# Projecting r and k of ten RWKV pairs with seven half products, from weight sums that transfers add up in device memory

## The reference, cut to what matters

```python
h = rmsnorm(x, g_pre)
p_shift, q_mem, gate = jnp.split(h @ w_in, RWKV_SPLITS, axis=-1)   # r, k, v (12 x 128 columns each), two small ones
prev = jnp.concatenate([shift_prev, p_shift[:, :-1]], axis=1)
s = p_shift + (prev - p_shift) * mu
r, k, v, wl, al = jnp.split(s, SHIFT_SPLITS, axis=-1)
...
y, wkv = wkv_recurrence(r_h, decay, k_mod, v_h, kk, a, wkv0)       # per head of 64
```

## Time and profile before

| | before |
|---|---|
| median of 3 runs | 1682.9 us |
| profiled execution / its span | 1686.12 / 1684.4 us |
| TensorE matmul busy | 1619.8 us (96%) |
| VectorE busy | 1022.2 us (61%) |
| ScalarE busy | 399.7 us (24%) |
| DMA | 419.97 MB, mean 249 GB/s |

### The profile page before, as it was taken

One profiled execution on the slowest core, in us unless ns is written; L12 is line 12 of the kernel. 1 busy time (PEld: TensorE's weight loads), 2 busy tenths in 40 slices (PEclk: granted clock), 3 DMA queues, 4 the chain that ended last, 5 costly groups with the idle time before them and its releaser, 6 DMA issues.

```text
span 1684.4 us, 28149 instructions
## 1 busy us (share of the span) xinstructions
PE 1619.8 (96%) x9704; PEld 1293.7 (77%) x9704; DVE 1022.2 (61%) x5017; ACT 399.7 (24%) x1011; POOL 160.8 (10%) x295
## 2 busy tenths in 40 slices
PE   7999999899999999998999989999999999999998
PEld 6667776677777777666996877777777777788997
DVE  4777455664555556435865376777777777432755
ACT  2122111211121212121112243333333333221012
POOL 1112211122122222221000000000000000020000
PEclk9999999999999999999999999999999999999999
DMA  9689999999999999998326043333333323365441
GB/s 382 247 318 395 416 408 401 363 387 420 412 406 420 419 409 413 403 382 340 118 88 257 30 158 123 104 104 104 104 104 104 104 85 113 119 255 193 151 159 52
DMA packets 102158, 419.97 MB, mean 249 GB/s; under 512 B 41844, under 2 KB 46464, under 8 KB 92416
## 3 DMA queue, kind: packets, MB, share of 16 engines
q0 software_dynamic: 41680, 218.91, 32.7%
q1 hardware_dynamic: 54264, 189.70, 29.8%
q10 hardware_dynamic: 6072, 9.56, 1.5%
HBM read 405.28 MB, written 12.85 MB: 248 GB/s over the span
## 4 chain that ended last, share of the span: by engine, by line
PE 77%; DVE 9%; DMA 7%; ACT 4%; issue 2%; POOLq 1%; POOL 0%; SPq 0%; ACTq 0%; DVEq 0%
PE psum L765 24%; PE psum L1203 11%; PE psum L837 10%; PE psum L819 6%; PE psum L1063 5%; DMA kvr<-in_cv 4%; PE psum L754 3%; PE psum L804 2%; PE psum L1250 2%; DMA kvr<-in_ck 1%; DVE arena L2403 1%; DVE kvr L1997 1%; PE psum L788 1%; PE psum L776 1%; ACT gT L1833 1%
## 5 line engine op out<-in xcount | busy, mean ns | idle before, releaser
L1997 DVE CUSTOM_DVE_ANT_0 kvr<-kvr,arena 128x128 f32<-128x128 f32 x1488 | 323.6, 288 | 110.5 <-DMA kvr<-in_ck 110.3
L765 PE MATMUL psum<-hT,wring 128*128 128x264 f32 x1536 | 363.5, 393 | 0.0
L765 PEld LDWEIGHTS psum<-hT,wring 128*128 128x128 f32 x1536 | 291.0, 193 | 67.4 <-issue 19.8
L1203 PE MATMUL psum<-hT,kvr 128*128 128x264 f32 x1152 | 283.9, 391 | 0.0
L1203 PEld LDWEIGHTS psum<-hT,kvr 128*128 128x128 f32 x1152 | 211.5, 190 | 34.4 <-issue 1.1
L1997 DVE DVE_READ_ACCUMULATOR2_ANT arena<- 128x1 f32 x1488 | 123.8, 83 | 0.0
L819 PE MATMUL psum<-hT,kvr 128*128 128x264 f32 x512 | 121.9, 389 | 0.0
L819 PEld LDWEIGHTS psum<-hT,kvr 128*128 128x128 f32 x512 | 94.6, 190 | 15.4 <-issue 0.4
L1063 PE MATMUL psum<-kvr,arena 128*32 128x384 f32 x1024 | 99.8, 505 | 5.4 <-DMA kvr<-in_cv 5.4
L699 POOL DMA_DIRECT2D kvr<-in_cv x128 | 67.7, 529 | 376.9 <-PE psum L1063 307.7
L699 POOL DMA_DIRECT2D kvr<-in_ck x128 | 67.6, 528 | 218.2 <-issue 217.5
(11 more groups left out here) (447 smaller groups left out, 2288.5 us busy)
## 6 DMA issues: line engine op xcount, KB each, us to landing
kvr<-in_ck POOLq DMA_DIRECT2D x128, 768.0 KB, 11.8
kvr<-in_cv POOLq DMA_DIRECT2D x128, 768.0 KB, 11.1
kvr<-in_wrkv SPq DMA_DIRECT2D x12, 3072.0 KB, 13.5
kvr<-in_wo SPq DMA_DIRECT2D x14, 2048.0 KB, 8.3
wring<-in_wkv SPq DMA_DIRECT2D x12, 2048.0 KB, 11.9
wring<-in_wm SPq DMA_DIRECT2D x8, 2048.0 KB, 12.5
wring<-in_wg SPq DMA_DIRECT2D x8, 2048.0 KB, 12.2
kvr<-in_wg SPq DMA_DIRECT2D x8, 2048.0 KB, 9.1
```

What stands on the lines that cost most here:

```text
L765: last = mm(psum[:, m % 2, 0:n], w[:, k, t * P:(t + 1) * P], rhs[:, k, 0:n], start=(k == 0), stop=(k == KT - 1))
L1203: last = mm(psum[:, m % 2, 0:T], w[:, k, t * P:(t + 1) * P], hT[:, k, :], start=(k == 0), stop=(k == KT - 1))
L1997: last = v_.tensor_tensor_reduce(page, page, qb[:, n % 2, h * P:(h + 1) * P], 1.0, 0.0, ALU.mult, ALU.add, S[:, n % 2, j * FH + h:j * FH + ...
```

## The change

For pairs 2 to 11 (turns 0 to 9), r and k are no longer two tiles of 16 k tiles and 264 columns. The weight block [first or second eight k tiles] x [r, k] and the inputs [k half] x [132-column half] form two 2x2 block matrices, multiplied with seven products of eight k tiles by 132 columns: R11, RS2, R12, RS1, RS4, RS3, R22. The v tile stays whole, in parts of 4, 4, 4, 2 and 2 k tiles. The seven products and five value parts are the twelve `project_part`s of a turn.

The four weight sums per pair are made by GpSimd's queue in device memory (`wsums`): four copies of 512 KB, then four adding transfers (`accum_op`) of 512 KB, three steps of which wait for the one before. Then nine half tiles of 512 KB (five from the weights in pieces of 512 bytes, four from the sums) are loaded by the same queue into a ring of twelve slots, instead of 3 MB by SyncE's. The sums of two pairs are made right after the last page of layer 0, the others two pairs ahead.

VectorE makes the four input sums once (in the place of the residual stream, which is stored to `xkept` and loaded back in turn 10), and in each turn joins products in five steps of 132 columns. ScalarE's copies are placed anew.

```diff
+SP0 = 2
+NSP = RP - SP0
+R11, RS2, R12, RS1, RVL, RS4, RS3, RVH, R22 = range(9)
+RSLOTS, RW1 = 12, 8 * P
...
 # SyncE
+            sp.wait_ge(sem("x_new"), len(RESIDUAL))
+            sp.dma_start(xkept, xT[:, :, :].rearrange("p k t -> p (k t)")).then_inc(sem("x_in2"), 16)
...
-                if o == RP - 3:
-                    late_unit(0)
                 if o == RP - 2:
                     late_unit(1)
                     late_unit(2)
-                if o + 3 < RP:
-                    sp.wait_ge(sem("p_done"), M_RKV + 3 * (o + 2))
-                    pair(o + 3, "wrkv", runit[:, (o + 1) % 2, :], f"proj_in{(o + 1) % 2}")
+                    sp.wait_ge(sem("x_in2"), 32)
+                    sp.dma_start(xT[:, :, :].rearrange("p k t -> p (k t)"), xkept).then_inc(sem("x_in2"), 16)
...
 # GpSimd
+            def sums_copied(i):
+                w = pair_weights(i)
+                for n, (k, x) in enumerate(((0, 1), (0, 0), (0, 0), (8, 0))):
+                    pool.dma_start(sum_at(i, n), w[:, k:k + 8, x, :]).then_inc(sem("rk_sum"), 16)
+            def sums_added(i, part):
+                w = pair_weights(i)
+                pool.wait_ge(sem("rk_sum"), 16 * (8 * i + (4, 6, 7)[part]))
+                if part == 0:
+                    pool.dma_start(sum_at(i, 0), w[:, 8:16, 1, :], accum_op=ALU.add).then_inc(sem("rk_sum"), 16)
+                    pool.dma_start(sum_at(i, 2), w[:, 0:8, 1, :], accum_op=ALU.add).then_inc(sem("rk_sum"), 16)
+                elif part == 1:
+                    pool.dma_start(wsums[i][:, 1, :], wsums[i][:, 0, :], accum_op=ALU.add).then_inc(sem("rk_sum"), 16)
+                else:
+                    pool.dma_start(wsums[i][:, 3, :], wsums[i][:, 1, :], accum_op=ALU.add).then_inc(sem("rk_sum"), 16)
+            def ring_load(i, j):
+                g = 9 * i + j
+                if g < RSLOTS:
+                    pool.wait_ge(sem("p_done"), M_RKV + 3 * (g // 6 + 1))
+                else:
+                    pool.wait_ge(sem("rk_mm"), g - RSLOTS + 1)
...
+            for i in range(NSP):
+                ring_load(i, R11)
+                if i + 2 < NSP:
+                    sums_copied(i + 2)
+                for j in (RS2, R12, RS1):
+                    ring_load(i, j)
+                if i + 2 < NSP:
+                    sums_added(i + 2, 0)
+                for j in (RVL, RS4, RS3):
+                    ring_load(i, j)
+                if i + 2 < NSP:
+                    sums_added(i + 2, 1)
+                for j in (RVH, R22):
+                    ring_load(i, j)
+                if i + 2 < NSP:
+                    sums_added(i + 2, 2)
...
 # TensorE
+                def half_product(j, out, x, first=True, last=True):
+                    w = ring_item(o, j).rearrange("p (k n) -> p k n", k=8)
+                    pe.wait_ge(*ring_full(o, j))
+                    for k in range(8):
+                        last_ = mm(out, w[:, k, :], x[:, k, :], start=first and k == 0, stop=last and k == 7, skip_group_check=True)
+                    last_.then_inc(sem("rk_mm"), 1)
...
 # VectorE
+                def joined_step(n):
+                    u2, w5 = pb[:, 1, 1:TH + 1], pb[:, 1, TH + 1:T + 1]
+                    dve.wait_ge(sem("rk_mm"), 9 * o + (2, 4, 6, 7, 9)[n])
+                    if n == 0:
+                        dve.wait_ge(sem("rk_a"), 5 * o + 1)
+                        last = tt(u2, rb, u2, ALU.subtract)
...
+                        if c == 3 * BLK // 4:
+                            joined_step(3)
```

More of the change, by code:

```diff
@@ L473, in few_slot @@
             layer, v = FEW[i]
-            return (v - PLAIN0) % 3 if layer == 0 else (v + 8) % 3
+            return (v - PLAIN0) % 3 if layer == 0 else (v + 10) % 3
         def late_full(v):
@@ L552, in trunk_step, with ring_item, ring_full @@
         vcols = nc.dram_tensor("vcols", (2, NS, 64), F32, kind="Internal").ap()
+        wsums = nc.dram_tensor("wsums", (NSP, P, 4, 8 * P), F32, kind="Internal").ap()
+        xkept = nc.dram_tensor("xkept", (P, KT * T), F32, kind="Internal").ap()
+        rsumT = xT[:, :, :].rearrange("p k t -> p (k t)").rearrange("p (s k t) -> p s k t", s=4, k=KT // 2)
+        ra, rv = psum[:, 0, 0:TH], psum[:, 0, TH:TH + T]
+        rb, rc, r7 = (psum[:, 1, n * TH:(n + 1) * TH] for n in range(3))
+        def ring_item(i, j):
+            at = (9 * i + j) % RSLOTS * RW1
+            return kvr[:, at:at + RW1]
+        def ring_full(i, j):
+            if j == R22:
+                return sem("pt_in"), 16 * (3 + i + 1)
+            return (sem(f"k_full{j}"), 16 * (K_FILLS + 2 + i + 1)) if j < 4 else (sem(f"v_full{j - 4}"), 16 * (V_FILLS + 2 + i + 1))
         block = ctx.enter_context(nc.Block())
@@ new lines, in _ @@
+            pool.wait_ge(sem("v_used"), NK)
+            for i in range(2):
+                sums_copied(i)
+                for part in range(3):
+                    sums_added(i, part)
+            for i in range(NSP):
[14 more added lines that the diff above has]
+                    sums_added(i + 2, 2)
@@ L813, in late_part @@
                 if quarter == 0:
+                    if part == 0:
+                        pe.wait_ge(sem("rk_a"), 5 * NSP)
+                        pe.wait_ge(sem("rk_j"), 5 * NSP + 1)
                     if t == 0:
@@ L1187, in turn_of, with value_part @@
                 w = runit[:, b, :].rearrange("p (k n) -> p k n", k=KT)
+                def half_product(j, out, x, first=True, last=True):
[4 more added lines that the diff above has]
+                    last_.then_inc(sem("rk_mm"), 1)
+                def value_part(k0, k1):
+                    j = RVL if k0 < 8 else RVH
+                    w = ring_item(o, j).rearrange("p (k n) -> p k n", k=8)
+                    if k0 % 8 == 0:
+                        pe.wait_ge(*ring_full(o, j))
+                    for k in range(k0, k1):
+                        last = mm(rv, w[:, k % 8, :], hT[:, k, :], start=k == 0, stop=k == KT - 1, skip_group_check=True)
+                    if k1 % 8 == 0:
+                        last.then_inc(sem("rk_mm"), 1)
@@ L1713, in own_share, with first_product, mixed_copies @@
                             .then_inc(sem("om_out"), 1)
+                seven = fill and o >= 0
+                def first_product():
+                    if seven:
+                        act.wait_ge(sem("rk_mm"), 9 * o + 1)
+                        ac(pb[:, 1, 1:TH + 1], ra, ACT.Copy).then_inc(sem("rk_a"), 1)
+                def mixed_copies(x):
+                    if not seven:
+                        return
+                    row = 3 * (o + 2) + x
+                    if x == 0:
+                        act.wait_ge(sem("om_out"), o + 3)
+                        act.wait_ge(sem("rk_a"), 5 * o + 2)
+                        act.wait_ge(sem("rk_j"), 5 * o + 4)
+                    elif x == 1:
+                        act.wait_ge(sem("rk_j"), 5 * o + 6)
+                    else:
+                        act.wait_ge(sem("rk_mm"), 9 * o + 8)
+                        ac(pb[:, 2, 1:T + 1], rv, ACT.Copy)
+                    ac(shout[:, row, :], rv[:, NPR - 1:T] if x == 2 else pb[:, x, NPR:T + 1], ACT.Copy)
+                    ac(pm[:, x, :], rv if x == 2 else pb[:, x, 1:T + 1], ACT.Copy, scale=om[:, b, x:x + 1]).then_inc(sem("rk_a"), 1)
                 def projected(t):
@@ L2342, in _ @@
                 weights(MH + FH + h, False, Pp1, rsum1, rinv1)
+                lo, hi = hT[:, 0:KT // 2, :], hT[:, KT // 2:KT, :]
+                t1, t2, t4, t3 = (rsumT[:, x, :, :] for x in range(4))
+                if h == 0:
+                    dve.wait_ge(sem("x_in2"), 32)
+                    dve.wait_ge(sem("h_out"), 28)
+                    ch.do(tt(t1, lo[:, :, 0:TH], lo[:, :, TH:T], ALU.subtract))
+                elif h == 1:
+                    ch.do(tt(t2, hi[:, :, TH:T], t1, ALU.add))
+                elif h == 2:
+                    ch.do(tt(t4, hi[:, :, 0:TH], t2, ALU.subtract))
+                else:
+                    tt(t3, lo[:, :, TH:T], hi[:, :, TH:T], ALU.subtract).then_inc(sem("rk_j"), 1)
             def turn_of(o):
@@ L2477, in turn_of @@
                     variances()
+                joined_step(0)
                 if prepare:
@@ L2484, in turn_of @@
                     normed()
+                joined_step(1)
                 if prepare:
@@ L2510, in turn_of @@
                     last.then_inc(sem("prepared"), 1)
+                    joined_step(4)
                 else:
```

107 lines of the change are left out of this document (100 added, 7 removed).

## The result

The changed kernel takes 1802.01 us (median of four runs, 1797.23 to 1807.91) against 1684.77 of the kernel before, run beside it: a ratio of 1.0701, 95% interval 1.0675 to 1.0727. I had expected 1677.2. The profiled execution took 1807.91 us, span 1806.2.

What follows compares the result with a forecast made beforehand. TensorE, busy 96% of the span, was taken as the bound. Half products -16.4, joins +2.7, late blocks +4 and turn 10 +4 gave -5.7 us: 1680.4 against the profiled execution, 1677.2 against the median; range 1667 to 1712.

Steps and rivals of the forecast that it cites:

- The likeliest case: Whole kernel: the forecast itself, 1677.2 us with its own range 1673 to 1682; chance 0.36.
- the second rival, late blocks: Near blocks' trip through device memory: each microsecond late over 1.29 of slack lengthens every turn; 1700 us; chance 0.20.
- TensorE's parts: TensorE's project parts: seven half products and the v tile save 1.64 us a turn, 16.4 us in ten turns.
- VectorE's joins: VectorE's five joins, 0.29 us each: only step 0 costs, 0.27 us a turn, 2.7 us in all.
- the rival of exposed weight loads: TensorE's seven half products: each starts with its weight load exposed, 2.7 us a turn, 1700 us; chance 0.06.
- Turn 10: SyncE's load of 2.16 MB back into xT ahead of vcols: 4 us, once; at most 5.7.
- The adding transfer: GpSimd's queue: costs between a copy and two reads; a pair's transfers take 26.5 to 32.6 us of engine time.
- the ring would have run dry: Rival: GpSimd's transfers of a pair outlast a turn and TensorE waits; 1722 us at 50 us a pair; chance 0.12.
- The near blocks: Their store and load, six pieces an engine: 0.4 us late a turn, 4 us in ten turns.
- The solved blocks: Their load back, 64 pieces: 3.8 us late against 3.6 of slack, met in the mean and missed at times.
- `vcols` no longer behind 3 MB: SyncE's queue: a reason for the undisturbed-turns rival (nothing else late, 1669 to 1673 us); chance 0.26.

Runs made afterwards that it cites:

- e12: Changed kernel without sums in the turns, every ring load from the first on moving one 4 KB row, products on junk weights: 1677.4 us, ratio 0.9956.
- e1: Changed kernel without the sums' copies and adding transfers for pairs 4 to 11, which read the sums of pairs 2 and 3: 1754.7 us, ratio 1.0399.
- e10: e1 with all nine ring loads of a turn held back to its last half product and issued together: 1768.7 us, ratio 1.0496.
- e15: e1 with three of the nine ring loads sent when the near blocks have landed, six when the solved ones have: 1691.5 us, ratio 1.0037.
- e4: Kernel before, plus a pair's eight sum transfers on GpSimd's queue in each of eight turns, read by nobody: 1782.9 us, ratio 1.0576.
- e3: Changed kernel with the adding transfers of pairs 4 to 11 made plain copies of the same pieces: 1781.8 us, ratio 1.0570.
- e5: Changed kernel, complete, with the stores of vcols issued ahead of the loads of vrkv and s0 on SyncE: 1822.6 us, ratio 1.0816.
- e8: e5 with all of GpSimd's transfers in rows of 4 KB, from weights laid out as half tiles: 1844.4 us, ratio 1.0946.
- e18: e16 with the four sum additions on VectorE, ahead of four of its idle places; complete: 1684.9 us, ratio 1.0005.
- e17: e16 with GpSimd's additions on 4 elements only, so the sums are junk: 1679.7 us, ratio 0.9973.
- e16: Changed kernel, complete, loading six half tiles a pair behind the solved blocks, GpSimd adding the four sums in the ring: 1700.0 us, ratio 1.0079.

## Why the prediction was wrong, step by step

It said 1677.2, with chances of 0.36 for faster, 0.29 for the same and 0.35 for slower; the time came 90 us above its range. The likeliest case failed and the mechanism of the second rival, late blocks, took its place, at seven times the price that I gave it. Not only its size was off: that rival's own rule, with the lateness that was measured (6.8 us), gives 10 x (6.8 - 1.29) - 9.7 = +45, and the rest came from other trips of the same chain and from the clock.

- **TensorE's parts and VectorE's joins: right.** Expected -16.4 + 2.7 = -13.7 us in ten turns; in e12, where only these are left, the last ten intervals have 14.7 less. The first is 2.0 longer (34.2 to 36.2), which no term of the sum had. The half products keep their length, so the rival of exposed weight loads fell: in e12, as in the changed kernel, the median record is 276 ns.
- **Turn 10: right.** I put 4 us for the residual's load; what lies behind the last reciprocal grew from 264.9 to 269.3 us in e12. That the load is what takes them is not shown apart.
- **The adding transfer: near the upper bound.** I took it between a copy (1.65 and 1.39 us of engine time for 512 KB) and one that reads twice (3.3 and 2.8). No row could show it. After, two of them in pieces of 512 bytes, alone on GpSimd's queue, from 801 to 813 us, and the middle of this, 807 to 811 us, in which SyncE's loads beside them are over:

```profile
q0 software_dynamic: 2080, 1.05, 69.7%
...
q0 software_dynamic: 1412, 0.71, 142.0%
```

The share adds up the times of the records. The first line gives 64 ns a record, 4.2 us of records an addition. But the second is over 100%, so records of one engine overlap there, and 1412 pieces in 4 us on 16 engines are 45 ns each, 2.9 us an addition, 1.8 copies. One in 4 KB rows took 60.4% of 5.5 us, 3.3 us, 2.4 copies. The Trainium skill, "Collectives: The Full Stack", in what it says of the reduce step, has it that an adding step reads two sources and writes one; the trace agrees roughly, with 2.9 us under two reads of 1.65 and 3.3 over two of 1.39. All of a pair's transfers then are 9 x 1.65 + 4 x 1.39 + 2 x 2.9 + 2 x 3.3 = 33 us, at the upper end of 26.5 to 32.6. In the turns their records took 84.3% of 300 us for 49.60 MB, 45 us a pair of 8.9 MB, overlap and waits for one another included. Whether the ring would have run dry in a turn of 39.7 us no run shows, since the turn had grown to 45 us and more by other means. The 20 us that adding costs are the smaller part of the loss.
- **The near blocks: the step that failed.** I gave them 0.4 us, from six pieces an engine at 60 ns in place of 35 to 43. Their trip became 6.8 us longer (9.8 instead of 3.0). Already e1, where the records of GpSimd's queue take 40% of the engines' time, has 5.4, 2.4 more. I scaled the delay with the number of a transfer's own pieces and checked it against the mean load. But the loads are not spread: each begins when a product ends, has 1.65 us and more for all 16 engines, and what falls into that comes late: with the same nine loads moved to other places the same trip takes 3.1 us (1.5 and 1.6, e10 and e15). The rule of the Trainium skill ("DMA: Bandwidth & Descriptors", Latency and other measured facts), which I weighed and set aside for the quiet row, 0.2 us for an access on average and 2 at high load, pointed the right way: the 3.6 us that it gave for the two trips lie between e1 and the change.
- **The solved blocks: size right by luck, weight wrong.** 3.8 us late was expected, 3.6 measured (5.8 instead of 2.2). But by my rule less load means less delay, and e1, whose queue has under half the record time, has 6.9: the rule doesn't hold, and the number met by chance. I let this pass because 3.6 us of slack stood against it "in the mean". The slack was gone as soon as `near` was late, since both are links of one chain.
- **One late trip or a chain of them.** I priced each small transfer for itself against its own slack. SyncE takes or awaits them in series: state store, `vcols`, broadcast, `near`, solved blocks, next turn. e4 shows the same chain late in the old order of work. "`vcols` no longer behind 3 MB" was no gain: it landed in 14.4 us before, and in 15.9 to 20.6 in the five turns from 1092 to 1372 us in which it stands in the chain of waits after.
- **The clock: not in the prediction.** After a stall TensorE's records come at half clock for some microseconds (1.97 instead of 1.09 us above), in e1 too: `from_state` at 1100.02 took 1.22 us behind 3.22 us of idle time, and 0.73 a turn earlier.
- **Against one another:** no transfers -7 us (e12), nine loads at the products' ends 71 + 7 = 78, the sums' copies and more 27 (e3 less e1), adding 20: together +118, measured +117. These are steps from one run to the next, so they must add up; in another order they would be sized otherwise (e4).

Open: what holds a small transfer back inside an engine. The runs exclude the bytes and GpSimd's queue as such as sole causes (e15) and show that a coincidence in time is needed; they do not tell whether it waits for pieces ahead of it on its engine or for the memory. Also open is how much of e5's and e8's extra loss is the later `vrkv`, and why e8's longer rows made it worse.

## What to carry to other kernels

A trip through device memory that stands in a chain is priced by what moves in the same microseconds, not by the mean DMA share: list where each small transfer is under way, and put bulk loads, by a semaphore, into the gaps between them (e1 to e15: 63 us for the same bytes). Price the chain of such trips, not each against its own slack. Before a saving on the busiest engine is believed, run the new order with its transfers taken out and the transfers with the old order; two runs (e12, e4) would have told here that the order is sound and the sums cost 99 us. Of the three ways to make the weight sums, additions on VectorE in its idle places were cheapest here (e18, 5 us over e17; GpSimd's 20): transfers that add took 1.8 to 2.4 copies each, and GpSimd's additions slow VectorE. And a record's time is not its price where the shares of a queue pass 100%.

## What the runs showed of the hardware

- The record of a 512-byte piece of an adding transfer in device memory lasts 64 ns, where a plain one lasts 25.7; records overlap on an engine, so that two such transfers together moved a piece per 45 ns and engine (807 to 811 us). In 4 KB rows one took 3.3 us per 512 KB, where a plain one takes 1.39 by the earlier trace rows.
- A transfer that GpSimd issues in 1024 pieces takes a median of 0.91 us of its time (914 ns, from 884 to 2277), not the 1.9 that I extended from the earlier trace rows.
- GpSimd adds 128x1024 float32 in 2477 ns, and while it does, VectorE's instructions with two SBUF inputs are held up: of 128x512, one lasted 2.83 us where it takes 0.69 (1154.06 in e16, beside additions from 1153.73 to 1159.10). The Trainium skill, "SBUF — State Buffer", section "SBUF: two separate sides", has this as an exclusive lock on a shared port pair; the trace agrees, also in that an instruction with a PSUM input is spared (1156.92 in e16, 0.69 us).
